# Layer 1 feed-forward: the first product as seven block products, and squares on VectorE alone

## The reference

```python
def _sq_relu_mlp(h, w1, w2):
    return jnp.square(jax.nn.relu(h @ w1)) @ w2
...
h_lat = h_lat + g1 * y_lat
h_lat = h_lat + g2 * _sq_relu_mlp(_modulate(_rms_norm(h_lat, norm2_g[i]), sh2, sc2), mlp_w1[i], mlp_w2[i])
```

## Time and profile before

| | |
|---|---|
| median of 3 runs | 2429.96 us (2429.19 to 2434.77) |
| span of the profiled execution | 2428.1 us |
| PE busy | 2281.3 us, 94% of the span |
| DVE busy | 1736.5 us, 72% |
| ACT busy | 1100.7 us, 45% |
| POOL busy | 1022.5 us, 42% |
| layer 1 feed-forward, pair 1 begins | 1799.28 us |
| one pair of the loop | 40.94 us |

### The profile page before, as it was taken

One profiled execution on the slowest core, in us unless ns is written; L12 is line 12 of the kernel. 1 busy time (PEld: TensorE's weight loads), 2 busy tenths in 40 slices (PEclk: granted clock), 3 DMA queues, 4 the chain that ended last, 5 costly groups with the idle time before them and its releaser, 6 DMA issues. The chain is left out here.

```text
span 2428.1 us, 36937 instructions
## 1 busy us (share of the span) xinstructions
PE 2281.3 (94%) x11598; PEld 1900.3 (78%) x11598; DVE 1736.5 (72%) x2835; ACT 1100.7 (45%) x1985; POOL 1022.5 (42%) x816
## 2 busy tenths in 40 slices
PE   5989979999999999999699799888999999999998
PEld 3768868888888888888687677766778888888887
DVE  5653787777777777777774688871688787878776
ACT  5553443333333333333443588882343444444443
POOL 0003623433333443333656476765435353545443
PEclk9999999999999999999799899999999999999999
DMA  7434112222222222222212211104111111121212
GB/s 272 176 130 174 66 35 70 86 87 72 84 78 69 70 82 98 69 80 88 105 53 109 81 36 34 35 22 191 44 35 53 51 46 57 37 67 35 69 35 96
DMA packets 79297, 192.75 MB, mean 79 GB/s; under 512 B 6896, under 2 KB 15472, under 8 KB 75888
## 3 DMA queue, kind: packets, MB, share of 16 engines
q1 hardware_dynamic: 76288, 184.92, 22.4%
q10 hardware_dynamic: 2928, 6.82, 0.8%
...
## 5 line engine op out<-in xcount | busy, mean ns | idle before, releaser
L862 POOL TENSOR_TENSOR ht<-ht,l_side 128x512 f32<-128x512 f32 x224 | 301.3, 1345 | 919.2 <-ACT l_side L971 910.8
L1275 DVE SCALAR_TENSOR_TENSOR ht<-l_yy_ps,mod,ht 128x512 f32<-128x512 f32 x672 | 466.1, 743 | 26.9 <-PE l_yy_ps L1591 26.0
L51 PE MATMUL l_z_ps<-nh,l_w1h 128*128 128x512 f32 (+1 forms) x1280 | 474.2, 370 | 11.7 <-DVE nl L1215 6.3
L52 PE MATMUL l_z_ps<-nl,l_w1h 128*128 128x512 f32 (+1 forms) x1280 | 473.2, 370 | 0.0
L53 PE MATMUL l_z_ps<-nh,l_w1l 128*128 128x512 f32 (+1 forms) x1280 | 472.6, 369 | 0.0
L1589 PE MATMUL l_yy_ps<-l_ah,l_w2h 128*128 128x512 f32 x896 | 355.6, 397 | 9.8 <-DVE ht L1275 6.9
L1590 PE MATMUL l_yy_ps<-l_al,l_w2h 128*128 128x512 f32 x896 | 351.0, 392 | 0.0
L1591 PE MATMUL l_yy_ps<-l_ah,l_w2l 128*128 128x512 f32 x896 | 350.5, 391 | 0.0
L971 ACT ACTIVATE l_side<-l_yy_ps,mod 128x512 f32<-128x512 f32 x224 | 154.1, 688 | 335.2 <-PE l_yy_ps L1591 335.2
L51 PEld LDWEIGHTS l_z_ps<-nh,l_w1h 128*128 128x128 f32 x1280 | 242.4, 189 | 54.5 <-issue 7.6
L53 PEld LDWEIGHTS l_z_ps<-nh,l_w1l 128*128 128x128 f32 x1280 | 242.5, 189 | 40.7
...
## 6 DMA issues: line engine op xcount, KB each, us to landing
l_aw<-ada SPq DMA_DIRECT2D x128, 256.0 KB, 2.9
l_w1f<-w SPq DMA_DIRECT2D x64, 512.0 KB, 3.5
l_w2f<-w SPq DMA_DIRECT2D x64, 512.0 KB, 4.9
...
queries<-qhl SPq DMA_DIRECT2D x16, 512.0 KB, 2.8
...
early<-fnet_w SPq DMA_DIRECT2D x11, 512.0 KB, 4.5
early<-wo SPq DMA_DIRECT2D x11, 512.0 KB, 3.5
```

The costliest lines, as they stand in the source:

```text
L51: pe.matmul(out, lh, rh, start=first, stop=False)
L52: pe.matmul(out, lh, rl, start=False, stop=False)
L862: pool.tensor_tensor(h, h, side[(i - 1) % 2][:], ALU.add).then_inc(s_add, 1)
L1275: dve.scalar_tensor_tensor(out=h, in0=y_ps[m][:], scalar=mod[:, layer, G2, c, 0:1], in1=h, op0=ALU.mult, op1=ALU.add).then_inc(s_acc, 1)
```

## The change

`layer_tail` is no longer called for layer 1; a new function `strassen_tail` takes its place. Layer 0 and everything ahead of the tail are as before.

- First product: the features are halved too, so the weights of a pair are a 2 x 2 grid of blocks and the tokens another. Seven block products of 4 chunks x 3 = 12 matmuls each take the place of eight: 84 matmuls. The right operands are three parts of the normed tokens and four sums or differences of them (`T1` to `T4` of the tokens, made once, ahead of pair 0, in full, high and low form). The left operands are three blocks of `w1` and four sums, made for each pair by POOL (`sum1`), and all seven are split again by ACT (`high1`) and POOL (`low1`), in tiles of 128x512.
- `z_ps` banks now gather several block products. ACT copies a bank out between two of them (`copied`), and DVE adds bank and copy (`zsum`) for `B11`, `B12`, `B22`. These three are then squared by one DVE step with both inputs in SBUF (`square`: max with 0, times itself). `B21` is read by ACT (relu) and squared by DVE as before.
- The order of the second product is M1, M6, M7, M4, M5, M3, M2; M1 stands ahead of the first product's last block product, the other six behind it.
- On POOL, the next pair's first weight splits and sums stand between this pair's adds.
- `w1` is loaded into the buffer `early`, 1 MB in one transfer; the rings of `w1` and `w2` splits have three places each.

```diff
-        layer_tail(nc, sem, sb, banks, 1, wo, early, s_pw, w1, w2, mod, meanw, eps, ident, nh, nl, ht, park=park, out=out)
+        strassen_tail(nc, sem, sb, banks, wo, early, s_pw, w1, w2, mod, meanw, eps, ident, nh, nl, nl_at, ht, park, out)
 
 
...
+    Z_ORDER = ["M1", "M2", "M5", "M6", "M3", "M7", "M4"]
+    Z_BANK = {"M1": 0, "M6": 0, "M7": 0, "M4": 0, "M2": 1, "M5": 2, "M3": 2}
+    Z_STARTS = ("M1", "M2", "M5")
+    W1_ORDER = ["A11", "A12", "S1", "S2", "S4", "S3", "A22"]
+    W1_PLACE = {"A11": 0, "S3": 0, "A12": 1, "S4": 1, "A21": 2, "S1": 2, "S2": 2, "A22": 3}
+    W1_SUM = {"S3": 1, "S1": 2, "S2": 3, "S4": 4}
+    TOK_OF = {"M1": "B11", "M2": "B21", "M5": "T1", "M6": "T2", "M3": "B22", "M7": "T3", "M4": "T4"}
+    Y_ORDER = ["M1", "M6", "M7", "M4", "M5", "M3", "M2"]
+    Y_STARTS = ("M1", "M5", "M2")
+    INTO = {"M5": (1, 1), "M3": (0, 1), "M2": (0, 0), "M1": (0, 0), "M6": (0, 1), "M7": (1, 1), "M4": (1, 0)}
+    W2_ORDER = ["A11", "S2", "S3", "A22", "S1", "S4", "A12"]
+    W2_PLACE = {"A11": 0, "S3": 0, "A12": 1, "A21": 2, "S1": 2, "A22": 3, "S2": 4, "S4": 4}
+    W2_SUM = {"S3": 1, "S2": 2, "S1": 3, "S4": 4}
+    ON_DVE2, ON_POOL2 = W2_ORDER[:4], W2_ORDER[4:]
+    A_ORDER = ["B11", "T2", "T3", "T1", "T4", "B22", "B21"]
+    A_BUF = {"B11": 0, "T2": 1, "T3": 2, "T1": 0, "T4": 3, "B22": 1, "B21": 2}
+    SLOT = {"B11": 0, "T1": 0, "B12": 1, "T3": 1, "B22": 2, "B21": 3, "T2": 4, "T4": 4}
+    T_AT = {"T1": 1, "T2": 2, "T3": 3, "T4": 4}
...
+                        sp.dma_start(w2f[:, 2 * h:2 * h + 2], w2[LAYER, rows, :, 512 * h:512 * h + 512].rearrange("c p n -> p c n")).then_inc(s_w2, 16)
+                def load_p(w):
+                    if w >= RING_P:
+                        low_done(sp, w - RING_P)
+                    sp.dma_start(pf[w % RING_P], wp[w % KC]).then_inc(s_pw[w % RING_P], 16)
+                for w in range(2, RING_P + 2):
+                    load_p(w)
+                load2(0, slice(0, 2))
+                sp.wait_ge(s_pl0, 1)
+                sp.wait_ge(s_pl, 1)
+                load1(0, slice(0, 1))
+                for w in range(RING_P + 2, UNITS):
+                    load_p(w)
+                def pair(p, row, rows):
+                    sp.wait_ge(s_w1l, p * 7 + (PRE + 7))
+                    load1(p + 1, row)
+                    sp.wait_ge(s_w2d, p * 4 + (PRE + 4))
+                    sp.wait_ge(s_w2p, p * 3 + (PRE + 3))
+                    load2(p + 1, rows)
+                pair(0, slice(1, 2), slice(2, 4))
+                with sp.Fori(1, PAIRS - 1) as p:
...
+                def second1(p):
+                    low1(p, 2)
+                    sum1(p, "S2", "A22", ALU.subtract, "S3", "S1")
+                    sum1(p, "S4", "A12", ALU.subtract, "S2", "A12")
+                def outputs(p, more):
+                    add(p, 0)
+                    if more:
+                        first1(p + 1)
+                    add(p, 1)
+                    if more:
+                        second1(p + 1)
+                    low2(p, "S1")
+                    add(p, 2)
+                    low2(p, "S4")
+                    add(p, 3)
+                    low2(p, "A12")
+                    for i in (4, 5, 6):
+                        add(p, i)
+                def pair(p, more):
+                    for i in (3, 4, 5, 6):
+                        low1(p, i)
+                    outputs(p, more)
...
+                def first_difference(j):
+                    d = t_full("T1", j)
+                    pool.wait_ge(s_tsum["T3"], j + 1)
+                    pool.tensor_tensor(d, d, t_full("T2", j), ALU.subtract).then_inc(s_tsum["T1"], 1)
+                def low_t(t, j):
+                    hi, lo = t_parts(t, j)
+                    pool.wait_ge(s_thi[t], j + 1)
+                    if t == "T3":
+                        pool.wait_ge(s_tsum["T2"], j + 1)
+                    lo_part(pool, lo, t_full(t, j), hi).then_inc(s_tlo[t], 1)
...
+                for j in range(HK):
+                    first_difference(j)
+                    low_t("T1", j)
+                    if j:
+                        low_t("T3", j - 1)
+                low_t("T3", HK - 1)
+                low1(0, 5)
...
+                        act.wait_ge(s_y, y_at(p, i - 3, 3))
+                    act.activation(w2h[:, i % 3], w2f[:, W2_PLACE[name]], ACT.Copy).then_inc(s_w2h, 1)
+                def copied(p, prod, to):
+                    act.wait_ge(s_z, z_at(p, prod))
+                    act.activation(slot[SLOT[to]][:], z_ps[Z_BANK[prod]][:], ACT.Copy).then_inc(s_cp, 1)
...
+                def pair_start(p):
+                    high2(p, "A11")
+                    act.wait_ge(s_al, p * 7 + PRE)
+                    copied(p, "M1", "B11")
+                    high1(p, 3)
+                    high1(p, 4)
+                    high(p, "B11")
+                def pair_middle(p, first):
+                    copied(p, "M5", "B22")
+                    high1(p, 5)
+                    if not first:
+                        high2(p, "S2")
+                        high2(p, "S3")
+                    copied(p, "M6", "B12")
+                    high1(p, 6)
+                    high(p, "T2")
+                    high(p, "T3")
+                    side_read(p, 0)
+                    high2(p, "A22")
+                    high(p, "T1")
+                def pair_end(p, more):
+                    act.wait_ge(s_z, z_at(p, "M4"))
+                    act.activation(slot[SLOT["B21"]][:], z_ps[0][:], ACT.Relu).then_inc(s_rl, 1)
+                    if more:
+                        high1(p + 1, 0)
+                        high1(p + 1, 1)
+                    high(p, "T4")
+                    side_read(p, 1)
+                    high2(p, "S1")
+                    high(p, "B22")
+                    if more:
+                        high1(p + 1, 2)
+                    side_read(p, 2)
+                    high2(p, "S4")
+                    high(p, "B21")
+                    side_read(p, 3)
+                    high2(p, "A12")
...
+                def third_sum(j):
+                    d = t_full("T3", j)
+                    dve.wait_ge(s_tn, KC + 2 * j + 2)
+                    dve.wait_ge(s_nl, KC + j + 1)
+                    dve.scalar_tensor_tensor(out=d, in0=d, scalar=dsh[:, j:j + 1], in1=plain(1, j), op0=ALU.add, op1=ALU.subtract).then_inc(s_tsum["T3"], 1)
...
+                def zsum(p, name, prod, n):
+                    s = slot[SLOT[name]][:]
+                    dve.wait_ge(s_z, z_at(p, prod))
+                    dve.wait_ge(s_cp, p * 3 + (PRE + {"B11": 1, "B12": 3, "B22": 2}[name]))
+                    dve.tensor_tensor(s, z_ps[Z_BANK[prod]][:], s, ALU.add).then_inc(s_x3, 1)
+                def square(p, name):
+                    s = slot[SLOT[name]][:]
+                    if name == "B21":
+                        dve.wait_ge(s_rl, p + (PRE + 1))
+                        src = z_ps[0][:]
+                    else:
+                        dve.wait_ge(s_x3, p * 3 + (PRE + ("B11", "B12", "B22").index(name) + 1))
+                        src = s
+                    dve.scalar_tensor_tensor(out=s, in0=src, scalar=0.0, in1=s, op0=ALU.max, op1=ALU.mult).then_inc(s_sqd, 1)
...
+                def pair_start(p):
+                    weights_start(p)
+                    zsum(p, "B11", "M2", 1)
+                    square(p, "B11")
+                    low(p, "B11")
+                    weights_more(p)
+                def pair_rest(p):
+                    zsum(p, "B12", "M3", 2)
+                    square(p, "B12")
+                    diff(p, "T1", "B12", "B11")
+                    zsum(p, "B22", "M7", 3)
+                    square(p, "B22")
+                    diff(p, "T2", "B22", "T1")
+                    diff(p, "T3", "B22", "B12")
+                    acc(p, 0, 0)
+                    low(p, "T2")
+                    acc(p, 0, 1)
+                    low(p, "T3")
+                    acc(p, 0, 2)
+                    low(p, "T1")
+                    low2(p, "A22")
+                    square(p, "B21")
+                    diff(p, "T4", "B21", "T2")
+                    acc(p, 1, 0)
+                    low(p, "T4")
+                    acc(p, 1, 1)
+                    acc(p, 1, 2)
+                    acc(p, 2, 0)
+                    low(p, "B22")
+                    acc(p, 2, 1)
+                    acc(p, 2, 2)
+                    acc(p, 3, 0)
+                    low(p, "B21")
+                    acc(p, 3, 1)
+                    acc(p, 3, 2)
+                    for i in (4, 5, 6):
...
+                for j in range(HK + 1):
+                    if j < HK:
+                        norm(1, j)
+                        norm(1, HK + j)
+                    if j:
+                        second_sum(j - 1)
+                        fourth_sum(j - 1)
+                    if j < HK:
+                        low_n(1, HK + j)
+                        third_sum(j)
+                    if j:
```

(30 more changed lines are left out.)

518 lines of the change are left out of this document (added).

## The result

The changed kernel takes 2540.6 us (median of 4 runs, 2540.2 to 2542.6), the kernel before 2432.0 beside it: 1.045 times as long, 95% interval 1.043 to 1.046. Predicted were 2545, with 2470 to 2575 as the range. The profiled execution has a span of 2538.5 us, 110.4 more than that of before.

A forecast was written before the change was run, and what follows sets the result against it. PE alone was taken to bound the loop. 30.5 us ahead of pair 1, 14 x (47.0 - 40.94) and -0.5 for the last pair gave +114.8 on 2428.1, 2542.9; with 1.9 for the median, 2545 us, range 2470 to 2575.

The forecast's parts named there:

- 14 pairs: Loop from pair 1 to pair 15: 47.0 us a pair in place of 40.94.
- last pair: Pair without a next w1: DVE's delays of 2.2 us against 2.73 saved, -0.5.
- POOL's nine steps: POOL's queue up to S1's weight split, from 6.85 to 20.7, making M5 7.1 us late in each pair.
- The cost of a step: POOL step 1.27 us; a collision with a DVE step with two SBUF inputs costs POOL 0.44.
- a lower overhead on SBUF: Three squares now reading SBUF: some 65 ns cheaper each, an estimated 0.2 us a pair.
- DVE's own order: Fourteen DVE steps to M6's first accumulation end at 9.7, PE wants the bank at 8.2; no extra cost.
- rival (2): Loop: POOL less late than DVE's order, M5 at 16.9, a pair 41.5, 2462 us; chance 0.08.
- The clock: In each pair, half clock behind the new 4 us wait for M5: eight matmuls slowed, 1.6 us added.
- Rival (1): Loop: POOL's chain holds M5 but the clock stays up, +90, 2520 us; chance 0.22.
- Ahead of pair 0: Token sums: 36.6 us of mutually exclusive DVE and POOL steps; pair 1 starts 30.5 later, bounds 20 to 38.
- The other side: Loop: PE stays the bound, S1's split through by 13.65, 38.2 a pair, 2411 us; chance 0.11.
- upper bound: Loop: 48.5 us a pair if ten collisions, not five, fall into POOL's chain.

The follow-up runs named there:

- POOL late: Changed kernel with all seven of POOL's next-pair w1 steps moved behind the last w2 split, ACT's S1 copy likewise; 2547.7 us, 1.048.
- fill run: Changed kernel with 18 unused matmuls into an unused bank ahead of the second product's M7, pairs 0 to 14; 2539.7 us, 1.0445.

## Why the prediction was right, and where it was not

| step | predicted | measured |
|---|---|---|
| pair 1 starts later by | 30.5 | 36.1 |
| first six block products end | 1799.2 | 1805.6 |
| 14 pairs | 84.8 (47.0 each) | 75.7 (46.35 each) |
| last pair | -0.5 | -1.4 |
| sum on the span | +114.8 | +110.4 |
| POOL's nine steps begin, end | 6.85, 20.7 | 6.95, 20.6 |
| M5 starts | 20.8 | 21.05 |
| M7 starts | 9.7 | 13.0 |
| matmuls at half clock, a pair | 8 | 11 |

**What costs.** The cost of a step, 1.27 us on POOL and 0.44 for each collision, and the rule that only DVE's steps with two SBUF inputs collide, carried the sum. The nine steps took 13.65 us in place of 13.85. The Trainium skill (SBUF — State Buffer, Who interferes with whom) says that a DVE instruction with two SBUF inputs contends with a GpSimd instruction that reads SBUF; the rows above agree, with 1.73 and 1.75 us on DVE for steps of 0.68, and 0.68 or 0.74 with an input in PSUM. Its other rule that the prediction weighed (Perfetto Trace Analysis, Optimizing Scalar/DVE Operations), a lower overhead on SBUF, gave nothing: undisturbed squares took 0.69 us from SBUF and 0.68 from PSUM. Where the kernel after is read by groups from 1900 to 2400 us, the lines of those squares are these (the second reads PSUM):

```profile
L2250 DVE SCALAR_TENSOR_TENSOR l_slot<-l_slot 128x512 f32<-128x512 f32 x31 | 30.2, 974 | 1.1
...
L2250 DVE SCALAR_TENSOR_TENSOR l_slot<-l_z_ps,l_slot 128x512 f32<-128x512 f32 x11 | 7.4, 677 | 0.0
```

**Wrong: which wait would be seen.** "PE waits once a pair, 3 to 5 us, for POOL's `l_w2l` (S1) ahead of the fifth product" did not happen; the visible wait ends on DVE's accumulation ahead of M7. The step that failed is DVE's own order, "at 0.6 to 0.7 they end at 9.7 with one collision ... and costs nothing on top". I gave POOL's chain five collisions and DVE's only one, though three of POOL's five (T1's low part, the `w2` split, T4's difference) are steps that stand in DVE's queue ahead of that accumulation: the fourteen steps met four. They ended at 12.8. Without three of those (POOL late) M7 started at 10.6, so 2.4 us are collisions and 0.9 is what my count was short of. By the prediction's own test, "the long wait ends on DVE's accumulation", this was rival (2), but rival (2) had M5 at 16.9 and 2462 us. Its wait came with the forecast's time, because the slow M7 moved PE to 21.0, beside POOL's 20.6. That the time agreed to 4 us in 110 is in part luck. It rests on this tie, and on two misses of opposite sign, 5.6 us too little ahead of pair 1 and 9.1 too much in the pairs. Still, the fill run, where M5 starts 0.10 us behind POOL's step at full clock and a pair is 46.28, shows that POOL's chain would have given this time by itself.

**The clock.** The fall to 0.50 behind a wait of 4.2 us came, for eleven matmuls, not eight: 2.4 us, not 1.6. It follows the wait for DVE and stands ahead of POOL's end, so it cost next to nothing by itself. The forecast had put its 1.6 us behind M5, where they would have counted in full; there the clock was 1.00. Small things made up half of that: M5 0.25 later, 8.6 us behind it for 8.19, and 16.55 for the 16.38 of six block products, most of it the wider spacing of the matmuls. Rival (1), 2520 with the clock up, was wrong for that reason: with the clock at 1.00 the fill run took 2539.7.

**Ahead of pair 0.** The reciprocal ended at 1756.7, predicted 1756.5; the first six block products ended at 1805.6, predicted 1799.2; pair 0 from there took 29.8, predicted 30.6. So the miss is the 6.4 ahead of it. 36.6 us in four rounds, 9.15 each, was worked out as a sum of steps that exclude each other. Measured are 9.88, and it is another thing: a chain through three engines with an idle 2.56 us on DVE. Three rounds of it make 2.2. With the idle time gone the round of 8.60 is DVE's own, with three collisions in it, so the exclusion was there, but it was not what set the time. Another 2.1 are a wait that I had not seen, PE, and the ACT step that ended just before:

```profile
1798.44 0.47 PE L2413 MATMUL l_z_ps<-nh,l_w1h 128*128 128x512 f32 x1 [2.12 <-issue]
...
1797.76 0.58 ACT L1996 ACTIVATE l_slot<-l_z_ps 128x512 f32<-128x512 f32 x1
```

ACT's copy of M5 out of its bank stands behind its high part of B11, and that behind DVE's square of B11, which comes after the last token step. Some 1.7 us more are lost by nine matmuls at half clock behind this wait (7.2 us for 24 matmuls that take 5.5). With ACT's token copies turned round the wait was 0.20.

**Two slips in the working.** The first of the three waits ahead of pair 0, 1.98 us, ends on POOL's `w1` low part and not on the norm or the squares. And five more collisions in POOL's chain at 0.44 add 2.2 us, which with the fall of the clock makes an upper bound of 49.2 us a pair, not 48.5. Neither changes the forecast.

**The other side.** PE as the bound at 38.2 a pair needed POOL's chain in 6.8 us. No run came near it: the shortest pair is 43.32, with the sums left out, and so with part of the work missing; with all of it, 44.70, with filling matmuls and three POOL steps moved. What holds even the 43.32 above 38.2 is, by its trace, PE's waits for `ht` (25.3 us in the 500 read) and the half clock behind them; no run takes these apart. That no order of the full work gets below the kernel before is not shown; five orders of POOL, DVE or both gave 46.05 to 47.62.
